# A recurrence's block inverse turned on VectorE instead of TensorE, and two projections split into three fp32r passes

## The chip, the cores and the metric

The program runs on one core of a Trainium2 chip. The metric is the device time of one execution in microseconds. TensorE multiplies, VectorE (DVE), ScalarE (ACT) and GpSimd (POOL) do the elementwise work, SyncE (SP) issues most transfers.

## The reference, cut to what matters

The program is a small network: an RWKV7 layer, a dense gated feed-forward, a pooling layer, a mixture of experts, an attention layer and a convolutional feed-forward. The change touches the RWKV7 recurrence and the output projections of the RWKV7 and the attention layer. The recurrence runs in two directions (d) over 256 context and 512 sequence positions, for 16 heads of 64:

```
def step(s, inp):
    r_t, w_t, kk_t, a_t, k_t, v_t = inp
    s_kk = jnp.einsum('bhvk,bhk->bhv', s, kk_t)
    s = (s * w_t[:, :, None, :] - s_kk[..., None] * (kk_t * a_t)[:, :, None, :]
         + v_t[..., None] * k_t[:, :, None, :])
    return s, jnp.einsum('bhvk,bhk->bhv', s, r_t)
...
return ((yn + bonus).astype(xg.dtype) * gate) @ w_o
```

The attention layer's projection is `mixed = concatenate([o_a, o_b]) @ w_out`. Both projections multiply 512 positions of 1024 features by a 1024x1024 fp32 matrix.

## The kernel before

The recurrence is worked in chunks of 64 positions, so a head has 12 chunks (n = 0 to 11), the first 4 of them context. Two heads share the 128 partitions, one on the upper and one on the lower 64, and both directions d are worked at once: this makes 8 head pairs (p = 0 to 7). A chunk's positions depend on each other through a 64x64 triangular matrix, whose inverse the kernel builds by doubling: blocks of 1 are inverted first, then five levels (lev = 0 to 4, `LAST` = 4) join neighbouring blocks, from 2 up to 64.

Every step is a name in one list, `plan`, and every engine works through its part of that list in order (`pairs`, lines 559 to 1247). The list is made of quads, four chunks at a time, three quads to a head pair. `quad(g)` writes the front steps of the four chunks of quad g, among them the link steps of the four chunks of the quad before:

- `score n`: TensorE (L951) makes the chunk's products, VectorE masks them into `LK` (L1225), and POOL adds the identity (L835) and masks a transposed start, `TB[..., 1, :]` (L838).
- `trans n`: TensorE transposes four operands (L967), ScalarE copies them (L1136). `akv n`: two products of the quad before (L1005, L1008), copied by ScalarE (L1145).
- `L n`: TensorE transposes the chunk's matrix (L973), VectorE masks it into the start `TB[..., 0, :]` (L1229).
- `X lev.n`: TensorE, L981; VectorE masks the result into `Xs` (L1233). `T lev.n`: TensorE makes the next inverse and its transpose: L991 gives `TB[..., 0, :]`, L993 gives `TB[..., 1, :]`, in the last level L993 alone; ScalarE copies both out of PSUM (L1142). X of the next level reads the former, T of the next level the latter.
- links: `U n` (L1017, L1020; ScalarE L1149), `Y n` (L1042 to L1046; ScalarE L1158) and `Z n` (L1027, L1029), which carry the state from chunk to chunk. Z's result goes through VectorE (L1243), which adds `Zs`, the decayed old state, which POOL makes (L844) after the Z before it. U of the next chunk waits for that.

Between these stand the feature steps of the next head pair and the output steps of the one before, spread evenly over the list by index. Those that matter: on VectorE scans (L1175), reciprocals in pieces of 128 columns (L1180 and L1196) and one L1183; on POOL, in the third quad, a row of large products (L768, L771, L775, L778, L781, L787, L790, L793) that ends in what the next head pair's scores read. On TensorE small stages of 384 or 512 columns (L858 and others).

The projections are `residual` (L1249): four chunks of weights are loaded into a ring of three buffers, `project` (L217) multiplies in fp32, VectorE adds the gated result to the residual (L1285), after ScalarE has scaled the residual (L1273). The feed-forward stages already use the class `Split`: ScalarE rounds a weight chunk to fp32r (`leading`, L144), VectorE takes the rest (`rest`, L151), and TensorE makes three products, hi·lo, lo·hi and hi·hi, in `Split.project` (L166 to L168).

## Time and profile before

| | us |
|---|---|
| median of 3 runs | 3656.8 (3654.11 to 3662.28) |
| the profiled execution | 3656.73 |
| its span | 3655.2 |
| recurrence, from its first scores to the last link | 343.4 to about 1188.6 |
| RWKV7 projection on TensorE | 1215.54, for 58.17 |
| attention projection on TensorE | 3128.32, for 57.52 |

The profiled execution agrees with the median within 0.1 us. Spans are in us from the span's start, durations in the group rows in ns. A matmul's row holds the time until its result is out, so neighbouring matmuls overlap in the profile, and what one costs TensorE is the distance from its start to the next one's start. An fp32 matmul is recorded as two instructions. A pair of 64x64 fp32 products for the two heads is four instructions.

### The profile page before, as it was taken

The numbers are of one execution on the slowest core, as the hardware profiler recorded it, in microseconds if no ns is written. First come the engines' busy times: TensorE is split into PE (matmuls) and PEld (weight loads), VectorE is DVE, ScalarE is ACT, GpSimd is POOL, SyncE is SP. The second block draws the span as 40 slices with busy tenths as digits, with TensorE's granted clock in tenths as the row PEclk, the third lists the DMA queues.
The fourth block names the chain that finished last, engine by engine and source line by source line (L and its number), as shares of the span: only waits on it lengthen the run. The fifth ranks groups of instructions, "written<-read, shape, count | busy, mean of one in ns | idle before, by whom it ended". The sixth has DMA issues, their size and how long they took to land. (4 is left out here: it accounts for less than half of the span.)

```text
span 3655.2 us, 76285 instructions
## 1 busy us (share of the span) xinstructions
PE 3171.5 (87%) x33165; PEld 2359.2 (65%) x33165; DVE 1706.7 (47%) x2615; ACT 1350.1 (37%) x1951; POOL 541.1 (15%) x629
## 2 busy tenths in 40 slices
PE   7998999999999779999449999999499766769989
PEld 3654888888888358844239999999243222357844
DVE  5412344433333147722638888888500456156610
ACT  1003555545554032200127777777201234133300
POOL 3003554445552010000000000000100110000000
PEclk9999999999999889999769999999799778889999
DMA  4631000000000167643039999998121000122221
GB/s 185 230 132 61 19 19 19 4 18 19 19 4 4 69 241 276 242 177 134 12 152 382 368 368 365 370 364 327 57 89 52 31 31 0 46 82 93 79 95 55
DMA packets 72490, 483.28 MB, mean 132 GB/s; under 512 B 10963, under 2 KB 12371, under 8 KB 30592
## 3 DMA queue, kind: packets, MB, share of 16 engines
q1 hardware_dynamic: 57824, 418.48, 30.3%
q0 software_dynamic: 12096, 52.43, 3.9%
q10 hardware_dynamic: 2304, 8.39, 0.6%
q8 instruction: 219, 3.59, 0.4%
q14 instruction: 47, 0.39, 0.0%
HBM read 457.73 MB, written 34.13 MB: 135 GB/s over the span
## 5 line engine op out<-in xcount | busy, mean ns | idle before, releaser
L2004 DVE TENSOR_TENSOR sb_moe_w_lo<-w_ring,sb_moe_w_hi 128x1408 fp32r<-128x1408 f32 (+1 forms) x132 | 255.2, 1934 | 66.8 <-ACT sb_moe_w_hi L1958 66.4
L1904 PE MATMUL ps<-sb_moe_w_hi,sb_x_feat_lo 128*128 128x352 f32 x832 | 274.3, 330 | 10.4 <-DVE sb_moe_w_lo L2004 10.4
L1906 PE MATMUL ps<-sb_moe_w_hi,sb_x_feat_hi 128*128 128x352 f32 x832 | 268.5, 323 | 0.0
L1905 PE MATMUL ps<-sb_moe_w_lo,sb_x_feat_hi 128*128 128x352 f32 x832 | 267.9, 322 | 0.0
L993 PE MATMUL ps<-sb_tb,sb_xs 64*64 64x64 f32 x3840 | 217.1, 222 | 24.1 <-DVE sb_xs L1233 24.1
L1142 ACT ACTIVATE sb_tb<-ps 128x256 f32<-128x256 f32 (+1 forms) x480 | 167.9, 361 | 105.2 <-PE ps L993 85.1
L1958 ACT ACTIVATE sb_moe_w_hi<-w_ring 128x2816 fp32r<-128x2816 f32 x80 | 204.1, 2553 | 0.1
L993 PEld LDWEIGHTS ps<-sb_tb,sb_xs 64*64 64x64 f32 x3840 | 187.0, 138 | 25.2 <-DVE sb_xs L1233 25.2
L991 PE MATMUL ps<-sb_xs,sb_tb 64*64 64x64 f32 x3072 | 186.7, 219 | 1.1 <-DVE sb_xs L1233 1.1
L166 PE MATMUL ps<-sb_conv_hl,sb_hi_conv_up 128*128 128x512 f32 x352 | 138.7, 394 | 35.4 <-DVE sb_lo_conv_up L151 35.4
L1904 PEld LDWEIGHTS ps<-sb_moe_w_hi,sb_x_feat_lo 128*128 128x128 f32 x832 | 157.0, 189 | 16.1 <-issue 15.4
L1904 PE MATMUL ps<-sb_moe_w_hi,sb_hid_feat_lo 128*128 128x256 f32 x572 | 163.2, 285 | 3.9 <-DVE sb_hid_feat_lo L2030 3.9
L217 PE MATMUL ps<-sb_chid,w_ring 128*128 128x512 f32 x352 | 153.4, 599 | 12.9 <-DMA w_ring<-w_down 12.9
L991 PEld LDWEIGHTS ps<-sb_xs,sb_tb 64*64 64x64 f32 x3072 | 158.6, 135 | 8.8 <-issue 6.4
L1505 PE MATMUL ps<-sb_hid,w_ring 128*128 128x512 f32 x352 | 155.6, 602 | 7.7 <-DMA w_ring<-w_ffn 7.7
L1906 PE MATMUL ps<-sb_moe_w_hi,sb_hid_feat_hi 128*128 128x256 f32 x572 | 161.8, 283 | 0.0
L1905 PE MATMUL ps<-sb_moe_w_lo,sb_hid_feat_hi 128*128 128x256 f32 x572 | 161.8, 283 | 0.0
L1243 DVE SCALAR_TENSOR_TENSOR sb_Z<-ps,sb_pend,sb_Zs 128x64 f32<-128x64 f32 x160 | 37.4, 275 | 265.5 <-PE ps L1029 218.3
L1458 PE MATMUL ps<-sb_ffn_hl,sb_hi_ffn_up 128*128 128x512 f32 x352 | 139.7, 397 | 22.2 <-DVE sb_lo_ffn_up L151 22.2
L1905 PEld LDWEIGHTS ps<-sb_moe_w_lo,sb_x_feat_hi 128*128 128x128 f32 x832 | 157.7, 190 | 0.0
L1906 PEld LDWEIGHTS ps<-sb_moe_w_hi,sb_x_feat_hi 128*128 128x128 f32 x832 | 157.0, 189 | 0.0
L981 PE MATMUL ps<-sb_tb,w_ring 64*64 64x64 f32 x3840 | 140.4, 219 | 11.6 <-ACT sb_tb L1142 7.8
(437 smaller groups left out, 7640.9 us busy)
## 6 DMA issues: line engine op xcount, KB each, us to landing
w_ring<-w_moe_up SPq DMA_DIRECT2D x67, 1408.0 KB, 8.5
sb_hm<-w_ada SPq DMA_DIRECT2D x48, 1024.0 KB, 7.0
w_ring<-w_ffn SPq DMA_DIRECT2D x22, 1024.0 KB, 4.9
w_ring<-w_up SPq DMA_DIRECT2D x22, 1024.0 KB, 4.7
sb_t_again<-w_moe_up SPq DMA_DIRECT2D x13, 1408.0 KB, 8.8
sb_hm<-w_moe_up SPq DMA_DIRECT2D x13, 1408.0 KB, 8.5
sb_b_again<-w_moe_up SPq DMA_DIRECT2D x13, 1408.0 KB, 8.1
w_ring<-w_moe_down SPq DMA_DIRECT2D x13, 1408.0 KB, 7.6
```

The costliest lines, as they stand in the source:

```text
L217: last = pe.matmul(ps[:, 2 * s + m, 0:width], ring.buf[s][:, at:at + P], moving(k), start=(k == 0), stop=(k == k_tiles - 1))
L981: last = pe.matmul(ps[hh, i, d * CH:(d + 1) * CH], M[hh, d, 0, :], tb[hh, d, 0, :], start=True, stop=True)
L991: pe.matmul(ps[hh, i, to:to + CH], tb[hh, d, 1, :], x2[hh, d, :], start=True, stop=True)
L993: last = pe.matmul(ps[hh, i, to + CH:to + 2 * CH], x2[hh, d, :], tb[hh, d, 1, :], start=True, stop=True)
L1142: S.activation(TB[:, s, i, :, lo:2, :], b[:, :, lo:2, :], ACT.Copy).then_inc(*act_f.did("t" + x[1:]))
L1458: pe.matmul(out, w_hi, HL[:, k, :], start=(k == 0), stop=False)
L1505: last = pe.matmul(ps[:, 2 * s, :], ring.buf[s][:, k * P:(k + 1) * P], HID[:, k, :], start=(k == 0), stop=(k == FT - 1))
L1904: pe.matmul(out, x_lo, w_hi, start=first, stop=False)
L1905: pe.matmul(out, x_hi, w_lo, start=False, stop=False)
L1906: return pe.matmul(out, x_hi, w_hi, start=False, stop=end)
L1958: S.activation(WH[:, s, :], raw[r], ACT.Copy).then_inc(rounded[s], 1)
L2004: return V.tensor_tensor(WL[:, s, w], raw[raw_at(c, i)[0]][:, w], WH[:, s, w].bitcast(F32), ALU.subtract)
```

## The change

First, the recurrence. `L n` goes. POOL's start `TB[..., 1, :]` is turned by VectorE's 32x32 block transpose into `TB[..., 0, :]` (`first n`). In levels 0 to 3, T makes only `TB[..., 0, :]` (64x64 per head and direction), and VectorE turns ScalarE's copy into `TB[..., 1, :]` (`turn lev.n`); the inverse is made of blocks of at most 32 up to that level. Level 4 makes only `TB[..., 1, :]`, as before. Second, `first`, `X`, `T` and `turn` are steps over two neighbouring chunks (n even), so that one mask, one copy and one turn serve 256 columns. Third, both projections use `Split`: the features (`x_hi`, `x_lo`) and each weight chunk are split, and TensorE makes three fp32r products.

```
-            out += [(p, f"L{n}") for n in cur]
+            out += [(p, f"first{n}") for n in cur[::2]]
...
+            turns = []
             for lev in range(LAST + 1):
                 for head in "XT":
-                    out += [(p, f"{head}{lev}.{n}") for n in cur]
+                    for n in cur[::2]:
+                        out.append((p, f"{head}{lev}.{n}"))
+                        if turns and (head == "X" or n % 4):
+                            out.append(turns.pop(0))
+                        if head == "T" and lev < LAST:
+                            turns.append((p, f"turn{lev}.{n}"))
                     if links:
                         out += links.pop(0)
...
-                        elif head == "L":
-                            pe.wait_ge(pool_f.sem, pool_f.at(f"I{n}", p))
-                            for d in range(2):
-                                for hh in heads:
-                                    to = P + d * CH
-                                    last = pe.matmul(ps[hh, i, to:to + CH], M[hh, d, 0, :], ident[hh, hh], start=True, stop=True)
...
                         elif head == "T":
                             pe.wait_ge(dve_f.sem, dve_f.at(f"x{lev}.{n}", p))
-                            if not lev:
-                                pe.wait_ge(pool_f.sem, pool_f.at(f"firstT{n}", p))
-                            for d in range(2):
-                                to = 256 + d * P
-                                if lev < LAST:
+                            if lev:
+                                pe.wait_ge(dve_f.sem, dve_f.at(f"turn{lev - 1}.{n}", p))
+                            else:
+                                pe.wait_ge(pool_f.sem, pool_f.at(f"firstT{n + 1}", p))
+                            for c in (i, i + 1):
+                                for d in range(2):
+                                    to = 256 + d * CH
                                     for hh in heads:
-                                        pe.matmul(ps[hh, i, to:to + CH], tb[hh, d, 1, :], x2[hh, d, :], start=True, stop=True)
-                                for hh in heads:
-                                    last = pe.matmul(ps[hh, i, to + CH:to + 2 * CH], x2[hh, d, :], tb[hh, d, 1, :],
-                                                     start=True, stop=True)
+                                        w, src = TB[hh, s, c, d, 1, :], Xs[hh, c, d, :]
+                                        if lev == LAST:
+                                            w, src = src, w
+                                        last = pe.matmul(ps[hh, c, to:to + CH], w, src, start=True, stop=True)
...
+                        elif head == "first":
+                            dve.wait_ge(pool_f.sem, pool_f.at(f"firstT{n + 1}", p))
+                            V.transpose(TB[:, s, i:i + 2, :, 0, :], TB[:, s, i:i + 2, :, 1, :]).then_inc(*dve_f.did(x))
+                        elif head == "turn":
+                            dve.wait_ge(act_f.sem, act_f.at(f"t{lev}.{n}", p))
+                            V.transpose(TB[:, s, i:i + 2, :, 1, :], TB[:, s, i:i + 2, :, 0, :]).then_inc(*dve_f.did(x))
...
             @block.tensor
             def _(pe):
-                project(pe, ring, ps, n, m_tiles, k_tiles, moving)
+                if split:
+                    pe.wait_ge(self.s_lo, self.parted + k_tiles)
+                    split.project(pe, ps, n, m_tiles, k_tiles, lambda k: split.x_hi[:, k, :], lambda k: split.x_lo[:, k, :])
...
             def _(act):
+                if split:
+                    for k in range(k_tiles):
+                        nc.scalar.activation(split.x_hi[:, k, :], split.whole[k], ACT.Copy).then_inc(self.s_hi, 1)
+                    split.leading(act, 0, 0)
...
             def _(dve):
+                if split:
+                    for k in range(k_tiles):
+                        dve.wait_ge(self.s_hi, self.parted + k + 1)
+                        V.tensor_tensor(split.x_lo[:, k, :], split.whole[k], split.x_hi[:, k, :].bitcast(F32),
+                                        ALU.subtract).then_inc(self.s_lo, 1)
+                    split.rest(dve, 0, 0)
```

Since the list is spread by index, and the front part of a quad has fewer names, other steps shift too. On POOL, in the third quad of a middle head pair, the order before was this (`sb_sg<-sb_a,sb_kk` is the first of the large products, `sb_Zs` is the decayed state of one link, `sb_t` is the input of the last feature stage):

```order
L768 TENSOR_TENSOR sb_sg<-sb_a,sb_kk 128x1536
L844 TENSOR_SCALAR sb_Zs<-sb_Z,sb_pend 128x64 x2
L771 TENSOR_TENSOR sb_ex<-sb_ex,sb_kk 128x1536
L844 TENSOR_SCALAR sb_Zs<-sb_Z,sb_pend 128x64 x2
L775 TENSOR_TENSOR sb_sg<-sb_sg,sb_Pi 128x1536
L844 TENSOR_SCALAR sb_Zs<-sb_Z,sb_pend 128x64 x2
L778 TENSOR_TENSOR sb_a<-sb_a,sb_k 128x1536
L781 TENSOR_TENSOR sb_Pi<-sb_a,sb_Pi 128x1536
L787 TENSOR_TENSOR sb_FR<-sb_cs,sb_r 128x1024
L790 TENSOR_TENSOR sb_t<-sb_a 128x512
L844 TENSOR_SCALAR sb_Zs<-sb_Z,sb_pend 128x64 x2
L793 TENSOR_TENSOR sb_t<-sb_t,sb_kq 128x512
```

And in the changed kernel:

```order
L780 TENSOR_TENSOR sb_sg<-sb_a,sb_kk 128x1536
L856 TENSOR_SCALAR sb_Zs<-sb_Z,sb_pend 128x64 x2
L783 TENSOR_TENSOR sb_ex<-sb_ex,sb_kk 128x1536
L787 TENSOR_TENSOR sb_sg<-sb_sg,sb_Pi 128x1536
L856 TENSOR_SCALAR sb_Zs<-sb_Z,sb_pend 128x64 x2
L790 TENSOR_TENSOR sb_a<-sb_a,sb_k 128x1536
L856 TENSOR_SCALAR sb_Zs<-sb_Z,sb_pend 128x64 x2
L793 TENSOR_TENSOR sb_Pi<-sb_a,sb_Pi 128x1536
L799 TENSOR_TENSOR sb_FR<-sb_cs,sb_r 128x1024
L802 TENSOR_TENSOR sb_t<-sb_a 128x512
L805 TENSOR_TENSOR sb_t<-sb_t,sb_kq 128x512
L856 TENSOR_SCALAR sb_Zs<-sb_Z,sb_pend 128x64 x2
```

The first `sb_Zs` stands where it stood. The second now has two large products ahead of it since the first, where it had one. The third stands behind `sb_a<-sb_a,sb_k`, where it stood ahead of it, and the fourth behind the last small product, where it stood ahead of it.

On VectorE, in the second quad's levels 0 and 1 and into level 2 (`sb_xs` are the masks of X, `sb_Z` the links, `sb_kk` and `sb_ysum` the reciprocals), before:

```order
L1233 TENSOR_TENSOR sb_xs<-ps,sb_mask_level 128x128 x4
L1180 RECIPROCAL sb_kk<-sb_kk 128x128
L1246 TENSOR_SCALAR sb_Z<-ps,sb_pend 128x64 x2
L1233 TENSOR_TENSOR sb_xs<-ps,sb_mask_level 128x128
L1180 RECIPROCAL sb_kk<-sb_kk 128x128
L1233 TENSOR_TENSOR sb_xs<-ps,sb_mask_level 128x128 x3
L1180 RECIPROCAL sb_kk<-sb_kk 128x128
L1243 SCALAR_TENSOR_TENSOR sb_Z<-ps,sb_pend,sb_Zs 128x64 x2
L1196 RECIPROCAL sb_ysum<-sb_ysum 128x128
L1233 TENSOR_TENSOR sb_xs<-ps,sb_mask_level 128x128 x3
L1196 RECIPROCAL sb_ysum<-sb_ysum 128x128
```

And changed (`STREAM_TRANSPOSE` is the turn):

```order
L1246 TENSOR_TENSOR sb_xs<-ps,sb_mask_level 128x256 x2
L1191 RECIPROCAL sb_kk<-sb_kk 128x128
L1243 STREAM_TRANSPOSE sb_tb<-sb_tb 128x4x64
L1260 TENSOR_SCALAR sb_Z<-ps,sb_pend 128x64 x2
L1191 RECIPROCAL sb_kk<-sb_kk 128x128
L1246 TENSOR_TENSOR sb_xs<-ps,sb_mask_level 128x256
L1243 STREAM_TRANSPOSE sb_tb<-sb_tb 128x4x64
L1246 TENSOR_TENSOR sb_xs<-ps,sb_mask_level 128x256
L1191 RECIPROCAL sb_kk<-sb_kk 128x128
L1243 STREAM_TRANSPOSE sb_tb<-sb_tb 128x4x64
L1207 RECIPROCAL sb_ysum<-sb_ysum 128x128
L1257 SCALAR_TENSOR_TENSOR sb_Z<-ps,sb_pend,sb_Zs 128x64 x2
```

A turn now stands between the masks, and each mask of two chunks is itself behind a turn or a reciprocal.

## Rows read from the trace of the kernel before

**Rows 1.** the page, busy time of an engine and its share of the span

```profile
PE 3171.5 (87%) x33165; PEld 2359.2 (65%) x33165; DVE 1706.7 (47%) x2615; ACT 1350.1 (37%) x1951; POOL 541.1 (15%) x629
```

**Rows 2.** windows: busy us (instructions) by engine, granted clock, DMA share, GB/s

```profile
330.00:1198.00 868.00, 802.63 (x23312) 734.52 (x23310) 327.36 (x987) 431.85 (x1008) 416.11 (x472) 0.97 0.04 13
650.60:689.10 38.50, 37.49 (x970) 32.13 (x968) 13.25 (x42) 19.82 (x44) 12.20 (x18) 0.99 0.01 3
689.10:719.60 30.50, 30.06 (x934) 28.01 (x930) 18.47 (x48) 13.82 (x37) 12.94 (x19) 1.00 0.02 4
719.60:756.70 37.10, 32.75 (x1034) 31.38 (x1032) 10.25 (x37) 21.82 (x51) 28.79 (x24) 0.96 0.13 42
754.90:760.70 5.80, 5.78 (x108) 5.78 (x110) 0.98 (x4) 1.83 (x6) 1.33 (x3) 0.50 0.01 3
1136.80:1168.00 31.20, 30.73 (x1045) 30.45 (x1040) 12.54 (x40) 14.38 (x39) 11.64 (x21) 1.00 0.02 4
```

**Rows 3.** timeline of TensorE: start us, us; first scores of the next head pair

```profile
756.69 0.42 PE L951 MATMUL ps<-sb_ex,sb_sg 64*64 64x64 f32 x4
```

**Rows 4.** groups by line in 330 to 1198: busy us, mean ns, idle before

```profile
L993 PE MATMUL ps<-sb_tb,sb_xs 64*64 64x64 f32 x3840 | 217.1, 222 | 24.1 <-DVE sb_xs L1233 24.1
...
L991 PE MATMUL ps<-sb_xs,sb_tb 64*64 64x64 f32 x3072 | 186.7, 219 | 1.1 <-DVE sb_xs L1233 1.1
...
L1142 ACT ACTIVATE sb_tb<-ps 128x256 f32<-128x256 f32 x384 | 143.8, 383 | 51.7 <-PE ps L993 33.8
...
L1233 DVE TENSOR_TENSOR sb_xs<-ps,sb_mask_level 128x128 f32<-128x128 f32 x480 | 111.4, 280 | 52.2 <-PE ps L981 52.2
...
L1180 DVE RECIPROCAL sb_kk<-sb_kk 128x128 f32<-128x128 f32 x42 | 39.6, 943 | 0.8 <-ACT sb_kk L1075 0.8
...
L1175 DVE TENSOR_TENSOR_SCAN sb_cs<-sb_scan_steps,sb_sg 128x256 f32<-128x256 f32 x42 | 28.7, 682 | 0.0
...
L973 PE MATMUL ps<-sb_consts,w_ring 64*64 64x64 f32 x768 | 27.7, 219 | 0.0
...
L1225 DVE TENSOR_TENSOR w_ring<-ps,sb_mask_score 128x256 f32<-128x256 f32 x32 | 13.6, 424 | 75.9 <-PE ps L951 75.9
```

**Rows 5.** timeline of TensorE, end of a third quad

```profile
748.03 0.33 PE L993 MATMUL ps<-sb_tb,sb_xs 64*64 64x64 f32 x4
748.15 0.33 PE L991 MATMUL ps<-sb_xs,sb_tb 64*64 64x64 f32 x4
...
754.92 1.97 PE L993 MATMUL ps<-sb_tb,sb_xs 64*64 64x64 f32 x32 [3.76 <-DVE sb_xs L1233]
```

**Rows 6.** timeline of POOL, first and last steps of that third quad

```profile
729.90 3.44 POOL L768 TENSOR_TENSOR sb_sg<-sb_a,sb_kk 128x1536 f32<-128x1536 f32 x1
...
753.24 0.85 POOL L844 TENSOR_SCALAR sb_Zs<-sb_Z,sb_pend 128x64 f32<-128x64 f32 x2
754.06 1.27 POOL L793 TENSOR_TENSOR sb_t<-sb_t,sb_kq 128x512 f32<-128x512 f32 x1
```

**Rows 7.** waits in 330 to 1198: us in total, times, longest us

```profile
DVE sb_Z L1243 <- POOL sb_Zs L844: 47.2, 7, 7.7
...
PE ps L993 <- DVE sb_xs L1233: 24.1, 8, 4.4
```

**Rows 8.** timeline of TensorE, both projections

```profile
1215.54 58.17 PE L217 MATMUL ps<-sb_b,w_ring 128*128 128x512 f32 x128 [21.31 <-DMA w_ring<-w_o]
...
3128.32 57.52 PE L217 MATMUL ps<-sb_b_again,w_ring 128*128 128x512 f32 x128 [11.07 <-DMA w_ring<-w_out]
```

**Rows 9.** timeline, start of the feed-forward that is split already

```profile
3226.51 1.91 ACT L144 ACTIVATE sb_hi_conv_up<-w_ring 128x2048 fp32r<-128x2048 f32 x1 [7.13 <-DMA w_ring<-w_up]
...
3228.45 2.29 DVE L151 TENSOR_TENSOR sb_lo_conv_up<-w_ring,sb_hi_conv_up 128x2048 fp32r<-128x2048 f32 x1 [7.77 <-ACT sb_hi_conv_up L144]
```

**Rows 10.** timeline of TensorE, the same stage in full run

```profile
3300.07 0.39 PE L166 MATMUL ps<-sb_conv_hl,sb_hi_conv_up 128*128 128x512 f32 x1
...
3310.27 0.39 PE L166 MATMUL ps<-sb_conv_hl,sb_hi_conv_up 128*128 128x512 f32 x1
```

More of the change, by code:

```diff
@@ L566, in pairs @@
         NG, LAST, H6, MASKS = N * QUADS, 4, TOK // 2, 12
+        FRONT = ("score", "trans", "first", "X", "T", "turn")
         SC_CUTS = ((0, 256), (256, 512), (512, 768))
@@ L639, in pairs @@
         plan += [("rec", *x) for x in quad(NG)] + [("output", N - 1, x) for x in outs]
-        fronts = [x for kind, p, x in plan if kind == "rec" and p == 0 and x.rstrip("0123456789.") in ("score", "trans", "L", "X", "T")]
+        fronts = [x for kind, p, x in plan if kind == "rec" and p == 0 and x.rstrip("0123456789.") in FRONT]
         links = [x for kind, p, x in plan if kind == "rec" and p == 0 and x not in fronts]
@@ L1046, in _ @@
                                     last = pe.matmul(ps[hh, 4, to:to + CH], Us[hh, d, :], M[hh, d, 1, :], start=False, stop=True)
-                        last.then_inc(*(pe_f if head in ("score", "trans", "L", "X", "T") else pe_c).did(x))
+                        last.then_inc(*(pe_f if head in FRONT else pe_c).did(x))
                 @block.scalar
@@ L1289, in _ @@
                 over_chunks(dve, n, body)
-        ring.end(n)
     def split_features(self, act, dve, HH, HL):
```

68 lines of the change are left out of this document (47 added, 21 removed).

## The prediction, made before the changed kernel ran

> **What bounds the kernel now.** The page comes first: TensorE is busy for 87% of the span [rows 1], so products taken from it count unless something else is late there. Then the windows. The recurrence is a quarter of the time, 868 us with TensorE busy for 803 [rows 2]. Its three quads differ. In the first and second quad of a middle head pair (650.6 to 689.1 to 719.6) TensorE is busy for 37.49 of 38.50 and 30.06 of 30.50 us: it is the bound. In the third (719.6 to 756.7) it is busy for only 32.75 of 37.10, and POOL for 28.79 [rows 2]. The timeline says why: the last T level starts at 754.92 after 3.76 us of idling for a mask [rows 5], and POOL works without a gap from 729.90 to 754.09, the end of the last sb_Zs [rows 6]. The chain is: sb_Zs late, so Z's VectorE step late, so the mask behind it in VectorE's queue late, so TensorE idle. The waits confirm that it is a habit: Z waits for sb_Zs 7 times, 47.2 us in total, and TensorE for the mask 8 times, 24.1 us, with 4.4 at the longest [rows 7]. So in the third quad POOL's large products are the bound, and after them TensorE runs at half its clock, granted 0.50 from 754.9 to 760.7 [rows 2].
>
> **The recurrence, what goes from TensorE.** Four 64x64 instructions (one product for two heads) take 0.117 us, the distance of two starts [rows 5], 29.2 ns each. L goes whole, 768 instructions, and of L993's 3840 only the last level's fifth stays, so 3072 go [rows 4]. That is 3840 x 29.2 ns = 112 us over 24 quads, 4.7 us a quad, all of it in a quad that TensorE bounds. On ScalarE 384 copies of 0.383 and 96 smaller ones become 240 of the former kind, and ScalarE was not the bound.
>
> **What comes to VectorE.** A mask of 256 PSUM columns is 0.424 (the same operation and width on another line) for two of 0.280 [rows 4], a gain. The turn, 128x256 from SBUF to SBUF, is in no row. From below, half of the mask's 0.280 [rows 4] would be 0.14; from above, the reciprocal's 0.943 for 128 columns [rows 4] doubled, 1.89, since that too is one input and one output. I take 0.40, nearest to the 0.424 of as many columns. The Trainium skill, "VectorE: DVE Perf Modes", section "The three transpose paths", gives 311 ns for a 128x128 bf16 turn and says that it turns 32x32 blocks only; by that an estimate for twice the columns lies between 0.31 and 0.62, and a sum with 0.62 would be some 15 us slower than mine. No run here shows it yet.
>
> First quad. One level of TensorE work was 3.7 us: X and the two halves of T at 32 instructions each, 0.93 each, and links of two times 0.47. It becomes 2.8. The shortest way round for one double chunk is X 0.47, then 0.22 until the result is out (the mean of a product [rows 4]), mask 0.42, T 0.47, 0.22 again, copy 0.38, some 0.1 of signals at each of four hand-overs: 2.6 us. It just fits, and the first quad has five small feature stages on TensorE besides, which give the slack back. VectorE needs per level two masks, two turns, a Z and a scan of 0.68 [rows 4], about 2.9 of some 4.2 us. So it keeps 4.7 less 0.8 for the scans' and the last level's waits (where no link stands between X and T): 3.9 us.
>
> Second quad. Here VectorE has nine reciprocals and the 1.0 us step in one queue with everything. VectorE works 18.47 us in it now [rows 2]. Following the new order: the last chunk's score mask ends 1 us after its products; POOL's two steps follow, but VectorE then has a reciprocal and a subtraction (0.94 and 0.7) ahead of the first turns, so the first X starts about 1.4 us later than TensorE could. In levels 0 to 2 a turn, a Z, a reciprocal and a mask stand in line between X and T. From the first X at 0 I get the first T of level 1 at 5.8, of level 2 at 9.4, of level 3 at 13.8 and of level 4 at 16.6, with the 1.0 us step ahead of the last mask, and the end at 18.8, where TensorE's own work is 14.0. That is 4.8 of waiting, and with 1.4 at the start and the 0.5 that it idled before, the 4.7 saved are gone: the second quad comes out at 30.5 again. I take 0, between -2.5 and +2.
>
> Third quad. POOL's line from its first large product to the last sb_Zs was 24.2 us (729.90 to 754.09), and the next scores came 2.6 later, at 756.69 [rows 3, 6]. POOL starts that line when the last chunk's score is masked, which doesn't change. In the new order the last small product, 1.27 [rows 6], stands ahead of the last sb_Zs: 25.5. Behind it come Z, mask, a second mask for the other double chunk and half a T, about as long as before. TensorE saves its 4.7 and waits them out, in two places, since the second sb_Zs now has two large products of 3.44 ahead of it. So +1 us, 0 to +3.
>
> Sum for the six middle head pairs: 6 x (-3.9 + 0 + 1) = -17.5. The first head pair has no output steps and its large products start a quad earlier: -3.5, -2.5 and -1 for its quads, -7. The last has no features, its third quad is bound by TensorE (30.73 of 31.20 us [rows 2]): three quads at 4.7 less 1.5, where loop and work are nearly equal, -9.5. Together -34.
>
> **The projections.** Each is 128 instructions in 58.17 and 57.52 us [rows 8]: 64 fp32 products at about 0.86, and some 3 us more for the half clock at its start. In three passes a product costs 3 x 0.2267 (45 distances in 10.20 us [rows 10]) = 0.68, so 64 take 43.5. Ahead of the first one now stand the rounding of the first weight chunk, 1.91, and the rest, 2.29, with a hand-over each: in the split stage the rest ends 4.2 us after the rounding starts [rows 9]; 4.4 with the wait. That is bare, since TensorE waits for exactly this chunk. The split of the features lies in the wait for that chunk (11 and 21 us [rows 8]). With 2.2 for the half clock: 50.1. The gain is 8.1 and 7.4, 15.4 together; later chunks need 4.2 of split against 10.9 of products each and are covered.
>
> **Rivals.** (a) VectorE isn't late: turns of 0.25 or shorter hand-overs, so that first and second quads of all eight head pairs keep their 4.7, and the third quads of the first and last. For it speaks that VectorE is busy for only 327 of 868 us [rows 2]; against it that its work comes in a line at the wrong moment. 18 x 4.7 = 85: 3656.7 - 15.4 - 85 = 3556. (b) POOL's new order costs more: the gap in the middle of the third quad and a longer one at its end keep the clock at half for longer, as after 754.9 [rows 2], about 6 us of products at half clock more for each of six head pairs, which is 3 us each: 3607 + 18 = 3625. The Trainium skill, "TensorE: Matmul & The Clock Gate", says that the clock follows recent activity of the array, so longer idling should mean more of it; the trace agrees with 0.50 behind a gap of 3.76 and 0.99 to 1.00 in quads without one. (c) Slower than before: the turn is the bound. In the second quad ten turns stand in line. Each 0.1 us over 0.40 costs 1 us there, 8 in all, and as much again in the first quads from about 0.8 on, where the spare 1.3 us of a level is used. At 0.9 the stage is even with the projections' gain, 3657; at 1.1, 3680. The reciprocal's row speaks for it, the scan's 0.68 for 256 columns [rows 4] against. (d) The three passes give nothing, as the start and a late second chunk eat them, and the recurrence does as I say: 3622.
>
> **Numbers.** The profiled execution, 3656.73, is 0.1 from the median, so the sum goes on it: 3656.7 - 34 - 15.4 = 3607. Chances: forecast 0.48 (3592 to 3622), (a) 0.18, (b) 0.17, (d) 0.07, (c) 0.10, of which half is above 3657. The range of 8 in 10 is 3565 to 3642. What can't be told from no change is 0.2%, 7 us. Faster 0.93, within 0.03, slower 0.04.
>
> **What would show it.** A turn's mean near 0.40; first quads of middle head pairs near 34.6, second near 30.5, third near 38, with two gaps in the third and POOL without one from its first large product; about 50 us from the first weight chunk's landing to each projection's last product. Wrong if second quads fall to 27 (a), if the windows' granted clock in third quads falls clearly below 0.9 and they exceed 40 (b), or if the turn's mean is above 0.8 (c).

## The result, and the profile after

The changed kernel takes 3616.95 us (median of 4 runs, 3614.81 to 3620.6) against 3659.54 for the kernel before in the same job (4 runs): a ratio of 0.9884, with a 95% interval of 0.9865 to 0.9904. The forecast was 3607, with a range of 3565 to 3642. The medians differ by 42.6 us, the profiled executions by less: the span falls from 3655.2 to 3619.0 us, by 36.2, and the profiled execution of the changed kernel is the slowest of its four. The recurrence, from its first scores to its last link, goes from 843.3 to 817.3 us (its last link ends at 1186.7 before, while the 1188.6 given ahead of the prediction is the start of the stage behind it), so 26 us come from there. The two projections give 15.5 between them. Some 5 us are given back in stages that the change doesn't touch: 2.6 ahead of the recurrence, which now starts at 346.0 instead of 343.4, and 5.2 between the two projections, against 2.5 won in others.

The recurrence first. The windows of the changed kernel are the whole of it and then the three quads of the fourth head pair, the pair that [rows 2] shows before. The columns are those of [rows 2].

```profile
346.00:1163.30 817.30, 710.99 (x19460) 638.73 (x19462) 387.31 (x886) 353.46 (x760) 399.39 (x467) 0.96 0.04 13
645.70:682.00 36.30, 34.60 (x814) 28.97 (x810) 16.91 (x38) 17.05 (x34) 13.18 (x18) 0.95 0.01 4
682.00:712.90 30.90, 26.52 (x770) 23.71 (x768) 21.36 (x44) 12.35 (x27) 11.53 (x19) 1.00 0.01 3
712.90:750.80 37.90, 29.09 (x876) 27.88 (x872) 12.11 (x32) 16.80 (x38) 28.79 (x24) 0.92 0.12 40
```

In the second quad TensorE is no longer the bound: it is busy for 26.52 of 30.90 us, where it had been 30.06 of 30.50. In the third, where it already waited before (32.75 of 37.10), it is busy for only 29.09 of 37.90. Over the six middle head pairs, from the first score of a quad to that of the next, the means are:

| | first quad | second quad | third quad |
|---|---|---|---|
| before | 39.0 | 30.5 | 37.05 |
| changed | 35.5 | 31.0 | 38.8 |
| difference | -3.5 | +0.5 | +1.8 |
| forecast | -3.9 | 0 | +1 |

The same window of the whole recurrence in the kernel before:

```profile
343.40:1186.70 843.30, 796.04 (x23301) 732.77 (x23302) 323.66 (x982) 426.62 (x1000) 401.52 (x467) 0.98 0.04 14
```

TensorE's busy time falls by 85 us, but it stands idle for 106.3 us where it had been 47.3.

The groups by line in 330 to 1165 (busy us, mean ns, idle before) answer to [rows 4]:

```profile
L990 PE MATMUL ps<-sb_tb,w_ring 64*64 64x64 f32 x3840 | 139.3, 219 | 19.5 <-DVE sb_tb L1240 11.5 <-ACT sb_tb L1151 8.0
L1005 PE MATMUL ps<-sb_xs,sb_tb 64*64 64x64 f32 x3072 | 116.6, 224 | 9.6 <-DVE sb_xs L1246 9.4
L1246 DVE TENSOR_TENSOR sb_xs<-ps,sb_mask_level 128x256 f32<-128x256 f32 x240 | 97.7, 407 | 45.5 <-PE ps L990 44.9
L1151 ACT ACTIVATE sb_tb<-ps 128x256 f32<-128x256 f32 x240 | 90.6, 383 | 137.8 <-PE ps L1005 133.6
L1243 DVE STREAM_TRANSPOSE sb_tb<-sb_tb 128x256 f32<-128x256 f32 x192 | 83.0, 432 | 75.8 <-ACT sb_tb L1151 75.0
```

The turn costs 0.432 us (forecast 0.40). The Trainium skill, "VectorE: DVE Perf Modes", section "The three transpose paths", gives 311 ns for a 128x128 bf16 turn. The estimate made from it for twice the columns was 0.31 to 0.62, and the trace lies within that. The mask of two chunks takes 0.407, as forecast from another line's 0.424. The row of L1005 is that of levels 0 to 3; the last level has a row of its own. What the links of L1257 wait for stands in the next view.

The waits in 330 to 1165 (us in total, times, longest us) answer to [rows 7]:

```profile
DVE sb_Z L1257 <- POOL sb_Zs L856: 64.6, 16, 6.4
...
PE ps L1005 <- DVE sb_xs L1246: 53.2, 36, 5.6
```

Z waits for POOL's `sb_Zs` 16 times instead of 7, for 64.6 us instead of 47.2. TensorE waits 53.2 us for masks, instead of 24.1. Of the 112 us of removed products the recurrence keeps 26; most of the other 86 went into such waits, since TensorE idles for 59 us more than before by the windows above. POOL's timeline in the third quad above, from its first large product on, shows what the links wait for:

```profile
722.79 3.45 POOL L780 TENSOR_TENSOR sb_sg<-sb_a,sb_kk 128x1536 f32<-128x1536 f32 x1
726.23 0.85 POOL L856 TENSOR_SCALAR sb_Zs<-sb_Z,sb_pend 128x64 f32<-128x64 f32 x2
727.05 3.44 POOL L783 TENSOR_TENSOR sb_ex<-sb_ex,sb_kk 128x1536 f32<-128x1536 f32 x1
730.45 3.43 POOL L787 TENSOR_TENSOR sb_sg<-sb_sg,sb_Pi 128x1536 f32<-128x1536 f32 x1
733.87 0.85 POOL L856 TENSOR_SCALAR sb_Zs<-sb_Z,sb_pend 128x64 f32<-128x64 f32 x2
...
745.95 1.26 POOL L805 TENSOR_TENSOR sb_t<-sb_t,sb_kq 128x512 f32<-128x512 f32 x1
747.19 0.86 POOL L856 TENSOR_SCALAR sb_Zs<-sb_Z,sb_pend 128x64 f32<-128x64 f32 x2
```

It works without a gap from 722.79 to 748.05, 25.3 us (before 24.2, forecast 25.5), and twice a small `sb_Zs` comes at the end of a stretch of large products; the one between them, at 738.10, has a single large product ahead of it. TensorE's timeline of the same quad, its idle times and the products behind them:

```profile
735.44 0.48 PE L1028 MATMUL ps<-sb_at,sb_tb 64*64 64x64 f32 x4 [3.19 <-DVE sb_Z L1257]
735.68 0.45 PE L1031 MATMUL ps<-sb_Z,sb_at 64*64 64x64 f32 x4
...
736.32 1.94 PE L1005 MATMUL ps<-sb_xs,sb_tb 64*64 64x64 f32 x32
...
740.66 1.11 PE L1005 MATMUL ps<-sb_xs,sb_tb 64*64 64x64 f32 x32
...
749.02 1.97 PE L1005 MATMUL ps<-sb_tb,sb_xs 64*64 64x64 f32 x32 [5.15 <-DVE sb_xs L1246]
750.77 0.42 PE L965 MATMUL ps<-sb_ex,sb_sg 64*64 64x64 f32 x4
```

These are the two gaps forecast, 3.19 and 5.15 us. Behind both the clock is at half: 32 instructions of L1005 take 1.94 us at 736.32 and 1.97 at 749.02, as in [rows 5], and 1.11 at 740.66, with no gap ahead of them. The next scores start 2.7 us after the last `sb_Zs`. Ahead of a third quad's first scores there is a smaller gap, of 1.66 us, ahead of the last T level of the quad before. It stands in all six middle head pairs. In four of them half the clock follows it, and these third quads have 39.2 to 39.4 us; in the other two the clock stays full, and they have 37.8 and 37.9. What decides between them is not shown. Two windows compare them, the time from the quad's first score to POOL's first large product, in one of the four and in the quad above:

```profile
816.80:828.20 11.40, 11.40 (x342) 11.34 (x338) 3.12 (x5) 7.17 (x14) 3.63 (x9) 0.86 0.02 4
712.90:722.80 9.90, 9.90 (x344) 9.86 (x338) 3.12 (x5) 7.19 (x14) 3.61 (x9) 1.00 0.02 5
```

As many instructions take 1.5 us more at a granted clock of 0.86, a mix of the two levels, than at 1.00.

Both projections, on the timelines of ScalarE, VectorE and TensorE (start, us), answer to [rows 8]:

```profile
1191.39 1.91 ACT L144 ACTIVATE sb_hi_wo<-w_ring 128x2048 fp32r<-128x2048 f32 x1 [5.73 <-DMA w_ring<-w_o]
1193.33 2.29 DVE L151 TENSOR_TENSOR sb_lo_wo<-w_ring,sb_hi_wo 128x2048 fp32r<-128x2048 f32 x1 [6.37 <-ACT sb_hi_wo L144]
1195.67 0.80 PE L166 MATMUL ps<-sb_wo_xl,sb_hi_wo 128*128 128x512 f32 x1 [24.82 <-DVE sb_lo_wo L151]
...
1240.64 0.39 PE L168 MATMUL ps<-sb_wo_xh,sb_hi_wo 128*128 128x512 f32 x1
...
3100.82 1.91 ACT L144 ACTIVATE sb_hi_wout<-w_ring 128x2048 fp32r<-128x2048 f32 x1 [1.03 <-DMA w_ring<-w_out]
...
3150.99 0.39 PE L168 MATMUL ps<-sb_wout_xh,sb_hi_wout 128*128 128x512 f32 x1
```

From the first chunk's landing (the start of its rounding) to the end of the last product it is 49.6 and 50.6 us, where it was 58.17 and 57.52: 8.6 and 6.9 less, 15.5 together, against 15.4 forecast.

### The profile page after: what moved, and what is told of

It reads as the page before. It is cut to its first block and busy times, and to the rows that moved or that the text cites. A ratio compares the mean times of both kernels' runs of the same rounds, so it can differ in the third digit from the quotient of the medians.

```text
span 3619.0 us, 68719 instructions
## 1 busy us (share of the span) xinstructions
PE 3070.7 (85%) x29453; PEld 2294.1 (63%) x29453; DVE 1801.1 (50%) x2543; ACT 1300.2 (36%) x1735; POOL 539.0 (15%) x629
## 5 line engine op out<-in xcount | busy, mean ns | idle before, releaser
L166 PE MATMUL ps<-sb_conv_hl,sb_hi_conv_up 128*128 128x512 f32 x352 | 138.5, 393 | 34.6 <-DVE sb_lo_conv_up L151 34.6
L217 PE MATMUL ps<-sb_chid,w_ring 128*128 128x512 f32 x352 | 153.3, 599 | 13.5 <-DMA w_ring<-w_down 13.5
L990 PEld LDWEIGHTS ps<-sb_tb,w_ring 64*64 64x64 f32 x3840 | 124.4, 135 | 35.2 <-DVE sb_tb L1240 14.5
L1236 DVE TENSOR_TENSOR w_ring<-ps,sb_mask_score 128x512 f32<-128x512 f32 (+1 forms) x96 | 57.8, 603 | 172.3 <-PE ps L965 172.3
L1151 ACT ACTIVATE sb_tb<-ps 128x256 f32<-128x256 f32 x240 | 90.6, 383 | 137.8 <-PE ps L1005 133.6
L1509 PE MATMUL ps<-sb_ffn_hh,sb_hi_ffn_up 128*128 128x512 f32 x352 | 137.7, 391 | 0.0
L1508 PE MATMUL ps<-sb_ffn_hh,sb_lo_ffn_up 128*128 128x512 f32 x352 | 137.7, 391 | 0.0
L167 PE MATMUL ps<-sb_conv_hh,sb_lo_conv_up 128*128 128x512 f32 x352 | 137.6, 391 | 0.0
```

Of the source, the lines that this page charges most:

```text
L166: pe.matmul(out, w_hi, lo(k), start=(k == 0), stop=False)
L217: last = pe.matmul(ps[:, 2 * s + m, 0:width], ring.buf[s][:, at:at + P], moving(k), start=(k == 0), stop=(k == k_tiles - 1))
L990: last = pe.matmul(ps[hh, c, d * CH:(d + 1) * CH], LK[hh, s, c, d, 0, :], TB[hh, s, c, d, 0, :], start=True, stop=True)
L1508: pe.matmul(out, w_lo, HH[:, k, :], start=False, stop=False)
L1509: last = pe.matmul(out, w_hi, HH[:, k, :], start=False, stop=(k == KT - 1))
```

## The experiments

Each total is a median beside the kernel before in the same job, and its ratio with the 95% interval is what is compared. For the recurrence the length is first scores to last link in the profile (843.3 before, 817.3 changed), and quads are means of the six middle head pairs.

One part of this length depends on the clock that the execution happened to get: the links of the last quad, behind the last T level, where TensorE has nothing else to do. Before, changed, and the changed kernel's same recurrence in e2:

```profile
1167.50:1186.90 19.40, 13.73 (x274) 12.07 (x269) 1.43 (x6) 3.82 (x13) 1.71 (x4) 0.74 0.01 2
1146.20:1163.50 17.30, 11.63 (x274) 10.10 (x270) 1.43 (x6) 3.86 (x12) 1.71 (x4) 0.90 0.01 2
1144.50:1165.60 21.10, 15.44 (x274) 13.62 (x270) 1.43 (x6) 3.85 (x12) 1.71 (x4) 0.62 0.01 2
```

As many instructions take 17.3 or 21.1 us, at a granted clock of 0.90 or 0.62. Over all runs this stretch has 16.0 to 22.1 us, so a difference of up to 5 us between two recurrences can come from it alone.

### Each half alone: e1_proj_only and e2_rec_only

The first is the kernel before with the split projections; the second is the changed kernel without them.

```
e1, of before:
-self.residual("wo", ..., ALPHA, load_x=self.A["xT"])
+self.residual("wo", ..., ALPHA, load_x=self.A["xT"], parts=True)      (wout alike)
e2, of the changed kernel:
-self.residual("wo", ..., ALPHA, load_x=self.A["xT"], parts=True)
+self.residual("wo", ..., ALPHA, load_x=self.A["xT"])                  (wout alike)
```

> The kernel before with the three-pass projections alone; the recurrence is the old one. Theory (the two parts add, each projection gains 7 to 9 us): 15 to 16 us faster than before, recurrence unchanged in length (about 845 us from first scores to last link). Rival (the split's start eats the gain, and the recurrence made more than its 26 us by its profile): within 7 us of before.

> The changed kernel with the projections in fp32 as before. Theory: the recurrence gains 26 us, so 24 to 28 us faster than before, quads of a middle head pair 35.3, 31.0 and 39.3 us. Rival (what the two medians differ by, 42.6, less 15.4 is the recurrence's): 27 or more; under 20 would say that part of its gain belongs to the projections.

Measured: e1 3644.09 beside 3657.17, ratio 0.9966 (0.9954 to 0.9978), 13.1 less by the medians and 12 by the ratio. e2 3637.14, ratio 0.9936 (0.9922 to 0.9951), 20.0 less by the medians and 23 by the ratio, with quads of 35.7, 31.0 and 38.8 and a recurrence of 822.1. Both lie a little under what was expected (15 to 16, and 24 to 28), within their intervals of 4 to 5 us to either side. Three passes for one fp32 product do save time, which rules out rival (d). By the ratios the halves make 36 us of the changed kernel's 42, and with such intervals nothing speaks against their adding up. The recurrences of e2 and of the changed kernel are the same code and differ by 5 us (822.1 and 817.3), 3.8 of them in the last links shown above.

### What holds the third quads: e3_zs_act

`sb_Zs` goes from POOL to ScalarE, right behind the copy of U.

```
-                        elif head == "U" and 0 < n < NCH - 1:        (POOL)
-                            pool.wait_ge(dve_c.sem, dve_c.at(f"z{n - 1}", p))
-                            for d in range(2):
-                                ... last = G.tensor_scalar(Zs[:, d, :], Zb[:, n % 2, d, :], PE2[...], None, ALU.mult)
+                            if 0 < n < NCH - 1:                      (ScalarE, behind U's copy)
+                                act.wait_ge(dve_c.sem, dve_c.at(f"z{n - 1}", p))
+                                for d in range(2):
+                                    ... last = S.activation(Zs[:, d, :], Zb[:, n % 2, d, :], ACT.Copy, scale=PE2[...])
```

> The changed kernel with sb_Zs, the decayed old state, made by ScalarE behind U's copy instead of by POOL; the rest of the order is the same. Theory (the third quad waits for sb_Zs behind POOL's large products, nothing else): the gaps before L1028 and before the last T level go, the third quads of middle head pairs fall from 39.3 to 32 to 34 us, then bound by the product that the next scores read; 30 to 43 us faster than the changed kernel. Rival (the third quad waits by its levels' hand-overs on VectorE, POOL merely runs beside): third quads stay above 37.5, gain under 10 us.

Measured: 3548.1 (3540.59 to 3552.49), ratio 0.9696 (0.968 to 0.9712): by the ratios some 69 us less than the changed kernel, for moving a step of 0.86 us. Third quads take 27.95 us, first ones 34.7, second ones 30.95; the recurrence 747.6. The windows of a second and a third quad:

```profile
653.40:684.40 31.00, 26.83 (x774) 23.89 (x770) 20.97 (x44) 13.44 (x33) 9.03 (x13) 1.00 0.01 3
684.40:712.20 27.80, 27.27 (x874) 25.96 (x870) 12.12 (x32) 18.10 (x46) 21.49 (x14) 1.00 0.18 54
```

In the third quad TensorE is busy for 27.27 of 27.80 us at a granted clock of 1.00, so here it is the bound now. The rival, hand-overs on VectorE with POOL merely beside them, is ruled out. ScalarE had room: its timeline there shows the step taking 0.57 to 0.59 us, between copies that it waits for anyway.

```profile
707.86 0.28 ACT L1154 ACTIVATE sb_Us<-ps 128x128 f32<-128x128 f32 x1 [1.59 <-PE ps L1025]
708.04 0.57 ACT L1160 ACTIVATE sb_Zs<-sb_Z,sb_pend 128x64 f32<-128x64 f32 x2
708.51 0.67 ACT L1145 ACTIVATE sb_tb<-ps 128x256 f32<-128x256 f32 x2
```

POOL's large products go on behind its back, five in a row with nothing between. The gain is more than the 30 to 43 us expected, since third quads were thought to come down to 32 to 34 us only. That they reach 28 could have been read ahead: TensorE's own 32.75 of [rows 2] less the 4.7 taken from it is 28.05.

### POOL's new order: e4_zs_order

POOL's old order in the third quads of the changed kernel.

```
+for p in range(1, N - 1):
+    for x, behind in (("GB", "U5"), ("Gkdk", "U6"), ("Gcoefin", "U7")):
+        plan.remove(("feature", p + 1, x))
+        plan.insert(plan.index(("rec", p, behind)) + 1, ("feature", p + 1, x))
```

> The changed kernel with POOL's steps of the third quads of head pairs 1 to 6 in the order of before (each sb_Zs ahead of the large product that it stood ahead of). Theory (the length is POOL's line up to the last sb_Zs, which one small product of 1.27 us lengthened): third quads 1.3 us shorter each, near 38, and the middle gap of 3.4 us smaller; 6 to 10 us faster than the changed kernel. Rival (c. 2 us more than before are half-clock products after the middle gap): with the middle gap gone the third quads are 37.1 again, 13 us faster. Rival (order is of no account): within 3 us.

Measured: 3608.5, ratio 0.9867 (0.985 to 0.9884), 8 us less than the changed kernel by the medians and 6 by the ratios, whose intervals overlap; third quads of 37.4 instead of 38.8. Like with like the difference is 1.2 us: 36.6 instead of 37.8 and 37.9 where the scores run at the full clock, 38.1 to 38.2 instead of 39.2 to 39.4 where they don't. That is the length of the small product (1.26) that had come ahead of the last `sb_Zs`, as expected. With the old order there is one gap of 7.0 to 7.8 us at the end instead of two, so the middle gap and the half clock behind it cost nothing of their own: POOL's line would have been waited for anyway. What rival (b) adds to the forecast's 1 us, 3 us of half clock by the new order, doesn't come back with the old one.

### What a change of values does: e5_short_rec

The four reciprocals of the output stage work on 1 of 128 columns; the other columns of the output's scale are left as they are, so this part of the computation is left out.

```
-                        return V.reciprocal(YS[:, 0, lo:hi], YS[:, 0, lo:hi])
+                        return V.reciprocal(YS[:, 0, lo:lo + 1], YS[:, 0, lo:lo + 1])
```

> The changed kernel with the four reciprocals of each output step (L1207) on 1 column of 128 instead of 128; the rest of the columns is left out of the computation. Theory (in the second quads VectorE's line of turns, masks and reciprocals is late for TensorE): four of nine large steps go there, the second quads of middle head pairs fall from 31.0 to 27.5 to 28.5 us, first and third quads stay; with the last head pair 15 to 25 us faster than the changed kernel. Rival (the second quads are bound by hand-overs between TensorE and ScalarE, VectorE has room): second quads above 30, gain under 6 us.

Measured: 3641.27 in total, which can't be used: other values reach the experts, whose products count 896 instead of 832 in the rows of TensorE, so the stages behind do other work. Only the recurrence ahead of it can be compared: 797.6 us, 19.7 less, with quads of 36.0, 28.4 and 37.8. The second quads fall by 2.5 us. So VectorE's line is what holds them, as the forecast had it, and not the hand-overs between TensorE and ScalarE; rival (a) has no support. The third quads are 1.0 shorter because none of the six starts at half the clock here. The window of one of them beside that of the changed kernel above:

```profile
673.90:702.30 28.40, 25.77 (x770) 23.45 (x768) 18.36 (x44) 12.16 (x26) 11.52 (x19) 1.00 0.01 3
```

VectorE's busy time falls by 3.00 us, and the quad by 2.50.

### The turn's price: e6_turn_twice and e7_pair_only

In e6 each turn is made twice (first into a buffer that nobody reads); in e7 the pairing of chunks stays, but TensorE makes both halves of T, and only POOL's start is turned by VectorE.

```
e6:
+                            V.transpose(TW2[:, lev, i:i + 2], TB[:, s, i:i + 2, :, 0, :])
                             V.transpose(TB[:, s, i:i + 2, :, 1, :], TB[:, s, i:i + 2, :, 0, :]).then_inc(*dve_f.did(x))
e7:
-                        if head == "T" and lev < LAST:               (the plan's turns)
+                        if False:
...
+                                    if lev < LAST:
+                                        for hh in heads:
+                                            pe.matmul(ps[hh, c, to:to + CH], TB[hh, s, c, d, 1, :], Xs[hh, c, d, :], ...)
```

> The changed kernel with each turn of levels 0 to 3 made twice, first into a buffer that nobody reads. Theory (a turn's 0.43 us is paid in full in second quads, partly in first ones, not at all in third ones, where POOL is the bound): second quads +3 us, first quads +1, third quads within 0.5; in all 20 to 35 us slower than the changed kernel. Rival (turns are hidden, VectorE is busy for half of the time only): under 8 us slower.

> The changed kernel without turns in levels 0 to 3: TensorE makes both products of T again, over two chunks, and one copy of 512 columns takes them out (first stays a turn). Theory (turns gain only where TensorE is the bound): first quads of middle head pairs near 39, second near 31, third near 38.8, the first and last head pair 8 and 10 us longer; 33 to 45 us slower than the changed kernel. Rival (the gain was the pairing's, fewer and larger instructions, and not the turns'): within 8 us of the changed kernel.

Measured: e6 3624.64, ratio 0.9909 (0.9893 to 0.9926), 7.7 us over the changed kernel by the medians and 9 by the ratios, whose intervals overlap; the theory had 20 to 35 and its rival less than 8. Quads of 35.5, 32.2 and 38.0. The groups show that the work was done:

```profile
L1244 DVE STREAM_TRANSPOSE sb_turned_again<-sb_tb 128x256 f32<-128x256 f32 x192 | 83.2, 433 | 60.6 <-ACT sb_tb L1152 60.5
L1245 DVE STREAM_TRANSPOSE sb_tb<-sb_tb 128x256 f32<-128x256 f32 x192 | 77.3, 403 | 0.0
```

So 80 us more of VectorE cost about 8, a tenth. The second quads pay 1.3 each, 7.7 in all, and the first and last head pair some 6. The third quads pay nothing for the turns, and here they are 0.8 shorter, 5 in all, since none of them starts at half the clock; without this the price would be about 13. The estimate that each 0.1 us of turn would cost 1 us in each second quad was three times too high: 0.40 us more would have been 4 us by it. Rival (c) falls with it: two turns in a row, 0.84 us, still leave the kernel 0.9% faster than before.

e7 3651.43, ratio 0.9978 (0.9966 to 0.9989), quads of 41.6, 30.3 and 36.3, recurrence 854.2. The total is as expected, 34 us over the changed kernel; that first quads take 41.6, where 39 was expected, and third ones 36.3, where it was 38.8, is not. Taking the turns' names out of the list spreads the side steps otherwise, and in the first quad of all six middle head pairs a feature stage of TensorE now stands where it has to wait for ScalarE:

```profile
453.97 1.95 PE L870 MATMUL ps<-sb_tw,sb_w_pair 128*128 128x384 f32 x4 [2.44 <-ACT sb_sg L1076]
```

Neither the kernel before nor the changed one has this wait. In four of the six half the clock follows it, and these quads have 42.1 us against 40.5. So the 11 us by which e7's recurrence is longer than 843.3 are not the price of pairing, and the 34 to 37 us against the changed kernel not those of the turns alone; a fair comparison of the two stands at e11.

### POOL's step alone, without the change: e8_before_zs

The edit of e3 on the kernel before.

> The kernel before with sb_Zs made by ScalarE instead of by POOL, all else as before. Theory (TensorE's own work is 32.7 us in a third quad of before, POOL's line of sb_Zs held it at 37.1): third quads 32.5 to 33.5, first and second within 0.5 of before, 22 to 30 us faster than before. Then the turned inverse is worth, without POOL's line, the distance from this kernel to the changed kernel with the same edit (3548.1), less 15 for the projections: 60 to 70 us, where with POOL's line it was 26. Rival (it was the new order alone that made sb_Zs costly): within 8 us of before.

Measured: 3623.9, ratio 0.9906 (0.989 to 0.9923), quads of 38.2, 30.5 and 32.6, recurrence 814.1. With it there is a table of four, in us of the recurrence:

| | both halves of T by TensorE | turned |
|---|---|---|
| `sb_Zs` on POOL | 843.3 | 817.3 |
| `sb_Zs` on ScalarE | 814.1 | 747.6 |

("Turned" is the whole change of the recurrence, pairing included.) Alone the two changes give 26 and 29, together 96; without the last links, whose length goes by the clock, 24, 31 and 97. As long as POOL's line stands, third quads can't use what is taken from TensorE; without it the change is worth 66. The totals agree: by the ratios e2 is 23 us less than before, e8 34 (22 to 30 were expected), and e3 111, of which the projections are 12 to 15. The rival, that only the new order made `sb_Zs` costly, is ruled out. The third quad's window of e8 shows TensorE as the bound already:

```profile
712.70:746.00 33.30, 32.32 (x1034) 30.90 (x1032) 10.75 (x37) 22.71 (x59) 23.87 (x16) 1.00 0.14 46
```

### Moving VectorE's work out of the second quad: e9_balanced, e10_balanced_pool, e12_rec_early

e9 is e3 with the side steps in another order: the features' products come earlier, and all output steps but the first, with their four reciprocals, go into the third quad. e10 is e9 with `sb_Zs` on POOL. e12 is e3 with three of the features' reciprocals ahead of the second quad's levels and `kkn` behind its last mask.

```
e9 (and e10), besides two names moved to the end of the features' list:
+                at = [x[2] for x in rest].index("GB")
+                mixed, rest, ended, last = ended[:1] + rest[:at], rest[at:-2], ended[1:], rest[-2:]
...
e12:
+                head = [f("Drec1"), f("Drec2"), f("Drec3"), o("Gy"), o("Pmean"), o("Dyc"), o("Asq"), f("Drec4"), o("Pvar"),
+                        f("Drec5"), o("Aroot"), *(o(f"Drec{i}") for i in range(4)), o("Gyn"), o("Aaff"), o("Gbonus"), o("Gated"),
+                        f("APx0"), f("Dkkn")]
...
```

> The changed kernel with sb_Zs on ScalarE (3548.1 us) and, on top, the order of the middle head pairs' side steps changed: the feature reciprocals come in the second quad's score phase, POOL's first two large products in the second quad's levels, and the output steps with their four reciprocals in the third quad. Theory (second quads are held by VectorE's line of nine reciprocals, third quads have room on VectorE): second quads 30.9 to 27.5 to 28.5, third quads within 1 of 28, first ones as they are; 12 to 20 us faster than that kernel, 3528 to 3536. Rival (third quads of 28 are bound by POOL's line up to the product that the next scores read, and the output steps' four POOL products lengthen it): third quads 30 or more, gain under 6 us.

> The changed kernel with only this other order of side steps, sb_Zs still on POOL. Theory (the line up to sb_Zs is POOL's; two of the large products now lie in second quads, where a late sb_Zs costs too): third quads fall from 38.8 to 31 to 34, second quads change by -2 to +2; 25 to 45 us faster than the changed kernel (3617). Rival (sb_Zs behind any 3.4 us product costs its wait wherever that stands, so that it only moves to the second quads): under 10 us.

> The changed kernel with sb_Zs on ScalarE, and the side steps of the middle second quads in another order: three feature reciprocals in the score phase, nothing of VectorE's ahead of the first turns, the 1.0 us step behind the last mask; third quads as they are. Theory (second quads lose 1.4 us at the first turns and about 0.9 for each reciprocal that stands between two masks; three of these go out of the line): second quads 30.9 to 28 to 29, first and third within 0.4; 10 to 18 us faster than 3548.1. Rival (what holds second quads is the way round a level, a reciprocal fits into it somewhere): second quads above 30.2, gain under 5 us.

Measured: e9 3579.68, ratio 0.9802 (0.9789 to 0.9816), quads of 34.6, 29.4 and 34.8: where 12 to 20 us less than e3 were expected, the recurrence is 30 us longer (777.1 and 747.6). Second quads give 1.5 and third ones take 6.8. The timeline of all engines in a third quad shows most of what went wrong:

```profile
718.29 1.26 POOL L825 TENSOR_TENSOR sb_ysum<-sb_ysum 128x512 f32<-128x512 f32 x1
719.58 0.81 ACT L1123 ACTIVATE sb_ysum<-sb_ysum,sb_params 128x512 f32<-128x512 f32 x1 [5.04 <-POOL sb_ysum L825]
720.30 0.26 ACT L1159 ACTIVATE sb_Us<-ps 128x128 f32<-128x128 f32 x1
...
720.61 0.48 PE L1052 MATMUL ps<-sb_FR,sb_Z 64*64 64x64 f32 x4 [3.56 <-ACT sb_Us L1159]
```

The output's affine step stands ahead of U's copy in ScalarE's queue and waits for POOL, and TensorE waits for the copy. It is the same fault as `sb_Zs` on POOL, with other names. The gap stands in all six third quads, and in five of them half the clock follows (35.0 us, against 33.6 in the sixth). The recorded rival had the size right (30 or more) but another way to it: POOL's last output product is done 7 us ahead of the next scores, so they don't wait for it. e10 3579.12, ratio 0.9794 (0.9781 to 0.9807), 34.7, 28.7 and 35.3, third quads a little over the 31 to 34 expected: in this order it no longer matters where `sb_Zs` stands, and even with POOL doing it the kernel is 33 to 38 us under the changed one (by the ratios, by the medians).

e12 3540.3 (3536.46 to 3545.24) beside 3660.67, ratio 0.967 (0.9657 to 0.9683), quads of 34.9, 30.75 and 28.5, recurrence 749.7. It has the lowest median of all, 3.3% under the kernel before, but that it is faster than e3 is not shown: the intervals of the ratios touch, and its recurrence is not shorter than e3's (747.6), so the 8 us between the medians, where 10 to 18 were expected, don't show where the steps were moved. Its second quads are not the 28 to 29 that VectorE's line promised, but what the rival had: three have 31.5 and three 30.0. TensorE's idle times of one of the latter:

```profile
759.64 1.12 PE L913 MATMUL ps<-sb_ysum,sb_consts 128*128 128x512 f32 x2 [1.67 <-POOL sb_ysum L825]
...
767.18 0.68 PE L1007 MATMUL ps<-sb_xs,sb_tb 64*64 64x64 f32 x16 [0.59 <-DVE sb_xs L1254]
...
770.90 0.68 PE L1007 MATMUL ps<-sb_xs,sb_tb 64*64 64x64 f32 x16 [0.56 <-DVE sb_xs L1254]
```

The waits of 1.15 ahead of the first X and of 1.38 ahead of the last T that e3 has in this place are gone, but a mean (L913) waits 1.67 us for POOL instead, which had not been there. It does so in all six, and in the three of 31.5 half the clock follows it (0.95 granted over the quad, 1.00 in those of 30.0). So this run doesn't test the theory cleanly: it took two waits away and put another in.

### One chunk or two: e11_single_turn

e3 with masks, copies and turns of one chunk each.

```
-            out += [(p, f"first{n}") for n in cur[::2]]
+            out += [(p, f"first{n}") for n in cur]
...
-                    for n in cur[::2]:
+                    for n in cur:
```

> The changed kernel with sb_Zs on ScalarE, but first, X, T and turn over one chunk each: twice as many masks, copies and turns of half the width. Theory (pairing pays by fewer fixed costs on VectorE, but lengthens the way round a level; where VectorE is late its gain is the larger): second quads 31.5 to 33, first quads 34 to 35, in all 5 to 15 us slower than with pairs (3548.1). Rival (run e7 had 11 us more than before in the recurrence with pairs and both products, so pairing costs): 5 to 15 us faster than 3548.1.

Measured: 3547.29 (3543.38 to 3555.66), ratio 0.9712 (0.9698 to 0.9726), against 0.9696 (0.968 to 0.9712) for e3. Quads of 36.75, 28.5 and 28.1. In the total the pairing is no gain and no loss, where the theory had a gain of 5 to 15 us and the rival as large a loss. By quads both are off: with single chunks the second quads are 2.5 us shorter, not longer, and the first ones 2 us longer. The latter can be read from a wait that is not the pairing's own. As in e7 the side steps are spread otherwise, and all six first quads have the wait of a feature stage:

```profile
541.10 1.56 PE L858 MATMUL ps<-sb_tw,sb_w_pair 128*128 128x384 f32 x4 [2.36 <-ACT sb_sg L1062]
```

The second quads are the more telling. All nine reciprocals are still in them, at about the same times, and the waits of 1.15 us ahead of the first X and 1.38 ahead of the last T that e3 has are gone: 28.5 us, as short as with four of the nine reciprocals cut down (e5). So by these two runs it takes both, reciprocals in VectorE's queue and steps over two chunks, to make that line late. Against e8, which has neither turns nor pairs, the ratio falls from 0.9906 to 0.9712, by 71 us, of which the projections are 12 to 15: turns without pairing, this wait included, are worth 56 to 59.

## Why the prediction was right, and where its sizes were off

**Which quad gains.** Right, and the heart of it. First quads gain 3.5 (forecast 3.9), second ones nothing (+0.5, forecast 0), third ones lose (+1.8, forecast +1). The mechanism of the second quad, VectorE's reciprocals in one queue with turns and masks, is shown by e5, with a condition that the forecast didn't see: with steps over one chunk the same queue is not late (e11). That of the third is shown by e3: with `sb_Zs` off POOL it goes to 28 us. The forecast's terms for the second quad, taken as they stand, don't make the zero that it took: 4.8 and 1.4 us of waiting, less the old 0.5 and the 4.7 saved, are +1.0. TensorE waits 1.15 us ahead of the first X and idles 4.4 in all, and the quad is 0.5 longer: the terms were a little too large, and the zero a little too small.

**The sum of the recurrence.** Its middle term was mis-sized: forecast -17.5 for the six middle head pairs, measured 6 x (-3.5 + 0.5 + 1.8) = -7.2, or -7.5 before rounding. Of the 10 us that are missing, 5 are in the third quads, four of which begin at half the clock, which the sum took in the rival alone; 3 are in the second and 2 in the first. The first head pair gave 5.0 (forecast 7). The last one gave 13.5 (forecast 9.5), and that is partly luck: its quads gave 3.3, 4.0 and 4.2 us up to the last T level, and 2.1 come from the last links, which had the full clock for longer than in the profile before (0.90 and 0.74). Together -26 in place of -34. The forecast's 3607 was 10 us too low by the median. The profiles put 8 of them here, but the two medians differ by 42.6 us and the two profiled executions by 36.2, so a few of these microseconds can't be placed.

**The turn.** 0.432 in place of 0.40, and the mask 0.407. Its effect in second quads was overrated: doubling it costs 1.3 us there, not 4 (e6). **The projections.** 15.5 in place of 15.4 by the profile, 12 to 13 by the totals of e1.

**The rivals.** (a) is ruled out: second quads of middle head pairs gain nothing, and e5 shows that VectorE's reciprocals hold them. That e3, at 3548, is close to its 3556 is by another way: first and third quads gain, the second ones still don't. (b) has its gaps and its half clock, but not its price. By its own signs it fails: third quads take 38.8 us and not over 40, and the clock of their windows is 0.92 and 0.89, where the kernel before had 0.96. The new order costs 1.2 us in a third quad (e4), which is the forecast's term; what comes on top, 1.4 us in four of the six, is half the clock behind a gap of the second quad, which e4 has too, in three of six. The Trainium skill, "TensorE: Matmul & The Clock Gate", section "What's actually happening", has the clock follow the array's recent activity. The trace agrees behind the gaps of 3.19 and 5.15 us, where 32 instructions take 1.94 and 1.97 us instead of 1.11; behind those of 1.66 us it was half in four cases and full in two. (c) and (d) are ruled out, by e6 and by e1.

**What it overlooked.** It named POOL's large products as the bound of the third quad and then took that as given. The reading was right, but moving a step of 0.86 us to another queue was worth more (69 us on top of the change) than the whole change (42).

## What to carry to other kernels

Before work is taken from the busiest engine, look at each stretch for the wait that ends last; if a small step of the critical chain stands in the queue of an engine with large side work, move that step first: here the two changes give 26 and 29 us alone and 96 together. Busy time less what is taken, as 32.75 - 4.7 here, says how short a stretch can get once its waits are gone. A step moved ahead in an in-order queue brings its own wait with it, as the affine step in e9 did. And where side steps are spread over a list by index, taking names out of the list or adding some moves all the others, so an experiment that does so tests two things: in e7 and e11 a wait of 2.4 us came in this way.

## What was not expected of the hardware

- The scan of 256 columns on VectorE takes 0.813 us on average in the changed kernel, where it took 0.682 [rows 4], with the same operands; what lengthens it was not tested.
- A block transpose of 128x256 fp32 takes 0.432 us, and 0.403 as the second of two in a row (e6).
- ScalarE makes both scaled copies of 128x64 in 0.57 us, where POOL needs 0.85 for them.
